# Mixture-of-experts router of a two-layer trunk: logits in four column groups, ranks by five products, gate products moved ahead, loads held back around the row stores and the gathers

## The reference

```python
scores = jax.nn.sigmoid(hf @ w_router)                 # 512 x 16
sel = (scores + router_bias).reshape(t, 4, 4)
group = jnp.argmax(jnp.sum(lax.top_k(sel, 2)[0], axis=-1), axis=-1)
...
_, local = lax.top_k(in_group, TOP_K)                  # two experts of the best group
gate = gate / jnp.sum(gate, axis=-1, keepdims=True)
order = jnp.argsort(flat_e)                            # assignments sorted by expert
...
y = (jax.nn.silu(xblk @ w_gate[e]) * (xblk @ w_up[e])) @ w_down[e]
out = jnp.zeros((t, d)).at[buf_tok].add(yb * buf_w[:, None])
x = x + g_f * out
```

## Time and profile before

| what | us |
|---|---|
| runs | 1720.21, 1727.75, 1726.51 (median 1726.51) |
| the profiled execution, its own time | 1720.86 |
| its span, first to last instruction | 1719.1 |
| PE busy in it | 1476.2 (86%) |
| DVE busy | 667.3 (39%) |
| ACT busy | 306.1 (18%) |
| mean granted clock of TensorE | 0.919 of full |

### The profile page before, as it was taken

How to read it: one execution, slowest core, us unless ns; L and a number is a source line. 1 busy time by engine, 2 the same in 40 slices (tenths; PEclk the granted TensorE clock), 3 DMA queues, 4 the chain that set the end, 5 groups by cost and what they waited for, 6 DMA issues and landing times.

```text
span 1719.1 us, 22464 instructions
## 1 busy us (share of the span) xinstructions
PE 1476.2 (86%) x9809; PEld 767.3 (45%) x9809; DVE 667.3 (39%) x1030; ACT 306.1 (18%) x498; POOL 73.2 (4%) x201
## 2 busy tenths in 40 slices
PE   5999999958887976999999599989559869999992
PEld 2445555437666434333333445655343343333331
DVE  1114433246774234332233235554572352233334
ACT  2121221133331030000000221211220300000002
POOL 7000000000000000000000100000000000000001
PEclk9999999969998996999999799989679878999997
DMA  9686662030001057898988610111000578989984
GB/s 334 201 290 228 213 201 93 1 147 3 3 3 51 0 234 289 345 413 318 428 332 330 246 60 26 49 49 50 0 1 0 211 299 336 418 331 406 370 322 167
DMA packets 91502, 335.21 MB, mean 195 GB/s; under 512 B 6552, under 2 KB 37516, under 8 KB 75020
## 3 DMA queue, kind: packets, MB, share of 16 engines
q1 hardware_dynamic: 76880, 287.94, 43.8%
q10 hardware_dynamic: 8476, 23.82, 3.5%
q0 software_dynamic: 6048, 22.02, 3.4%
HBM read 310.70 MB, written 23.07 MB: 194 GB/s over the span
## 4 chain that ended last, share of the span: by engine, by line
PE 73%; DVE 12%; DMA 8%; ACT 5%; issue 1%; POOL 0%; ACTq 0%; DVEq 0%; SPq 0%; POOLq 0%
PE banks L1629 18%; PE banks L1228 15%; PE banks L1651 10%; PE banks L1558 7%; DVE work L1765 4%; PE banks L1261 3%; PE banks L1217 3%; PE banks L1164 3%; DMA work<-in_w_down_dram 2%; DMA work<-h_rows,idx_tok 2%; DMA h_rows<-y_features 2%; PE banks L1612 2%; DVE work L1771 2%; DVE ring L1765 1%; DMA ring<-in_w_ada_dram 1%
## 5 line engine op out<-in xcount | busy, mean ns | idle before, releaser
L1228 PE MATMUL banks<-h_features,ring 128*128 128x512 f32 (+1 forms) x656 | 290.7, 598 | 4.0 <-ACT h_features L865 4.0
L1629 PE MATMUL banks<-ring,work 128*64 128x512 f32 x672 | 236.1, 613 | 2.3 <-issue 2.3
L1629 PE MATMUL banks<-work 128*64 128x512 f32 x512 | 212.3, 595 | 0.0
L1228 PEld LDWEIGHTS banks<-h_features,ring 128*128 128x128 f32 (+1 forms) x656 | 121.4, 189 | 156.1 <-issue 152.7
L1765 DVE TENSOR_TENSOR work<-work,banks 128x256 f32<-128x256 f32 (+2 forms) x90 | 48.5, 561 | 199.3 <-PE banks L1629 145.5
L1558 PE MATMUL banks<-y_features,ring 128*128 128x512 f32 x256 | 115.2, 613 | 8.6 <-DVE small L2246 8.6
L1651 PE MATMUL banks<-work 128*64 128x512 f32 x320 | 112.7, 593 | 0.0
L1765 DVE TENSOR_TENSOR work<-work 128x512 f32<-128x512 f32 (+10 forms) x205 | 103.3, 504 | 14.4 <-ACT work L1054 3.6
L1629 PEld LDWEIGHTS banks<-ring,work 128*64 128x64 f32 x672 | 71.8, 141 | 72.9 <-issue 69.1
L1651 PE MATMUL banks<-ring,work 128*64 128x512 f32 x256 | 98.4, 592 | 0.0
L1629 PE MATMUL banks<-h_features,work 128*64 128x512 f32 x192 | 91.4, 624 | 2.2 <-ACT work L1087 2.2
(11 more groups left out here) (355 smaller groups left out, 1870.1 us busy)
## 6 DMA issues: line engine op xcount, KB each, us to landing
ring<-in_w_up_dram SPq DMA_DIRECT2D x16, 2048.0 KB, 13.0
y_features<-in_w_ada_dram SPq DMA_DIRECT2D x28, 1024.0 KB, 5.6
work<-in_w_down_dram SPq DMA_DIRECT2D x14, 2048.0 KB, 15.8
ring<-in_w_gate_dram SPq DMA_DIRECT2D x12, 2048.0 KB, 11.0
work<-in_w_up_dram SPq DMA_DIRECT2D x10, 2048.0 KB, 13.2
work<-in_w_gate_dram SPq DMA_DIRECT2D x10, 2048.0 KB, 13.1
ring<-in_w_ada_dram SPq DMA_DIRECT2D x8, 2048.0 KB, 11.8
h_features<-in_w_gate_dram SPq DMA_DIRECT2D x8, 2048.0 KB, 9.1
```

Of the source, the lines that this page charges most:

```text
L1228: ins = mm(PS[0:w, b, :], lhsT=W[:, k, c0:c0 + w], rhs=h[:, k, :], start=(k == 0), stop=(k == KD - 1))
L1629: ins = mm(PS[rows, bank, :], lhsT=xt[:, k, rows], rhs=ws[lane][:, k, :], start=(k == 0), stop=(k == KD - 1))
```

## The change

Seven things are changed; both layers run all but the last, which is made once.

1. The logits go to four column groups of 32 columns: tile k goes to group k mod 4, with a 32-wide stationary operand (the 16 columns of tile k and those of k+1, of which only the first 16 count). ACT copies the full bank, and PE adds the four groups while it turns the tokens, by a product with `quarter_sum` (a 128x16 matrix with four ones in a column). ACT takes the Exp of the 128x64 result, before its four row copies.
2. The ranks are five products over `both` as one 80-column operand, padded with zeros, in place of 14.
3. The gate products stand ahead of the wait for the choices, and go to banks 5 and 6.
4. `tokens_of_blocks` stands inside the first round's gate product, after five of its eight steps, where it stood behind all eight.
5. SP waits for the four row stores ahead of load 4 (down weights of expert 0), where it issued it at once.
6. SP waits for gather 1 ahead of load 6, where it waited for gather 0.
7. Constants for the first point are made once at the start (five DVE instructions).

```diff
@@ SP
                     if place < 2:
+                        if part == 2 and place == 0:
+                            sp.wait_ge(sem(f"l{l}_rows_stored"), 16 * NT)
                         src = ws[part][l, place:place + 1]
...
                                 sp.wait_ge(sem("table_ready"), l + 1)
-                                sp.wait_ge(gathered[l][0], 16)
+                                sp.wait_ge(gathered[l][1], 16)
@@ ACT experts
                 act.wait_ge(sem("logits_ready"), 2 * l + 1)
-                act.activation(sgt[0:E, :], PS[0:E, 4, :], ACT.Exp, scale=-1.0).then_inc(sem("logits_exp"), 1)
+                act.activation(sgt, PS[:, 4, :], ACT.Copy).then_inc(sem("logits_exp"), 1)
+                act.wait_ge(sem("logits_ready"), 2 * l + 2)
+                act.activation(sc, PS[:, 7, 0:NT * E].rearrange("p (a b) -> p a b", b=E), ACT.Exp, scale=-1.0)\
+                   .then_inc(sem("logits_exp"), 1)
...
-                act.activation(gate_row, PS[:, 0:2, :], ACT.Copy).then_inc(sem("scaled"), 1)
+                act.activation(gate_row, PS[:, 5:7, :], ACT.Copy).then_inc(sem("scaled"), 1)
@@ PE experts
-                    ins = mm(PS[0:E, 4, :], lhsT=wr[:, k, :], rhs=h[:, k, :], start=(k == 0), stop=(k == KD - 1))
+                    g = k % 4
+                    ins = mm(PS[32 * g:32 * g + 32, 4, :], lhsT=wr[:, k:k + 2, :].rearrange("p a b -> p (a b)"),
+                             rhs=h[:, k, :], start=(k < 4), stop=(k >= 4))
...
-                            ins = tr(PS[:, 7, s * E:(s + 1) * E], sgt[0:E, s * P:(s + 1) * P], ident[0:E, 0:E])
+                            ins = mm(PS[:, 7, s * E:(s + 1) * E], lhsT=sgt[:, s * P:(s + 1) * P], rhs=quarter_sum,
+                                     start=True, stop=True)
...
-                pe.wait_ge(sem("choices_ready"), 3 * l + 1)
-                for t in range(NT):
-                    for s in range(t + 1):
-                        mm(PS[:, 5, t * E:(t + 1) * E], lhsT=(upper if s == t else ones), rhs=both[:, s, :],
-                           start=(s == 0), stop=(s == t))
-                for s in range(NT):
-                    ins = mm(PS[:, 5, NT * E:(NT + 1) * E], lhsT=ones, rhs=both[:, s, :], start=(s == 0), stop=(s == NT - 1))
-                ins.then_inc(sem("rank_ready"), 1)
-                pe.wait_ge(sem("rows_copied"), NT * l + NT - 1)
                 for k in range(KD):
-                    ins = mm(PS[:, k // 4, (k % 4) * P:(k % 4 + 1) * P],
+                    ins = mm(PS[:, 5 + k // 4, (k % 4) * P:(k % 4 + 1) * P],
                              lhsT=mod[:, l, 40 + k:41 + k].to_broadcast([P, P]), rhs=ident, start=True, stop=True)
                 ins.then_inc(sem("comb_turned"), 1)
+                pe.wait_ge(sem("choices_ready"), 3 * l + 1)
+                every = both_padded.rearrange("p a b -> p (a b)")
+                mm(PS[:, 4, 0:(NT + 1) * E], lhsT=upper, rhs=every, start=True, stop=False)
+                for later in range(1, NT + 1):
+                    ins = mm(PS[:, 4, later * E:(NT + 1) * E], lhsT=ones, rhs=every[:, 0:(NT + 1 - later) * E],
+                             start=False, stop=(later == NT))
+                ins.then_inc(sem("rank_ready"), 1)
...
                     lanes_up(0, ws, xTb[r % 2], range(5))
                     if r:
                         turn_act(r - 1)
+                    else:
+                        tokens_of_blocks()
                     lanes_up(0, ws, xTb[r % 2], range(5, KD)).then_inc(sem(f"l{l}_gate_done"), 1)
                     if r:
...
-                    else:
-                        tokens_of_blocks()
@@ DVE choose
-                dve.wait_ge(sem("logits_ready"), 2 * l + 2)
-                link(tsc(sc, PS[:, 7, 0:NT * E].rearrange("p (a b) -> p a b", b=E), 1.0, ALU.add))
-                link(dve.reciprocal(sc, sc))
+                link(dve.memset(both_padded[:, NT, :], 0.0))
+                dve.wait_ge(sem("logits_exp"), 2 * l + 2)
+                sigmoid_tail(sc)
```

More of the change, by code:

```diff
@@ L192, in trunk @@
         alup = small(256)
-        wr = small(8, E)
+        wr = small(9, E)
+        quarter_sum = small(E)
         rs = work[:, 20480:20992]
@@ L305, in trunk @@
         oh = ro(2, NT * E)
-        both = ro(NT, E)
+        both_padded = ro(NT + 1, E)
+        both = both_padded[:, 0:NT, :]
         gk = ro(2, NT)
@@ L2310, in choose @@
                 dve.wait_ge(sem("rank_ready"), 3 * l + 1)
-                link(tt(rank, PS[:, 5, 0:NT * E].rearrange("p (a b) -> p a b", b=E), both, ALU.subtract))
+                link(tt(rank, PS[:, 4, 0:NT * E].rearrange("p (a b) -> p a b", b=E), both, ALU.subtract))
                 link(stt(rank_first, both[:, :, 0:2], -1024.0, rank[:, :, 0:2], ALU.mult, ALU.add))
```

15 lines of the change are left out of this document (11 added, 4 removed).

## The result

The changed kernel takes **1709.2 us** (median of 8 runs, 1703.8 to 1713.2), the kernel before took 1726.1 beside it (8 runs, 1715.0 to 1728.4). The ratio is 0.991, with a 95% interval of 0.9885 to 0.9936: 11 to 20 us faster. The forecast was 1704, the range 1692 to 1716.

A forecast was written before the change was run, and what follows sets the result against it. Bound: each layer's router waits between the last normalised tile and round 1. Gains of 8.8 + 1.0 = 9.8 us a layer, 19.6 in both, took 1720.86 to 1701.3, placed at 1704 towards the run median; range 1692 to 1716.

The forecast's parts named there:

- Logits: Router logits in four column groups: only the last tile's product remains behind ACT's last tile, ending 3.0 us earlier.
- Ranks and gate products: Router: ten rank instructions take 2.0 us, not 5.7; moving the gate products saves 2.3; first rows known 8.0 earlier.
- Row stores: Before gather 0: without loads 4 and 5 in the way, the last store lands 10.9 us earlier, at 646.0.
- Gather 0: Ahead of round 0: released by the first rows at 646.9, takes 9.7 us beside loads, lands 5.0 earlier.
- Gather 1 and load 6: Ahead of round 1: gather takes 4.4 us, not 11.25; PE waits 2.1 for load 6; round 1 starts 8.8 earlier.
- Clock: Round 1's start: of 2.6 us lost to the low clock, 1.0 a layer is won back.
- thin cover: Loads in later rounds: the tightest one's slack shrinks from 8.4 to 3.6 us, still enough that PE does not wait.
- little contention: Rival: gather 0 needs only 4.4 us and the clock stays up; about 1690 us; chance 0.12.
- the column groups in line: Rival: the logits' column groups do not run beside each other, losing 3.0 us a layer; 1710 us; chance 0.04.
- Full contention: Rival: gather 0 takes 11.3 us and the clock falls as before; about 1709 us; chance 0.16.
- The stream of loads: Rival: loads starting 4.7 us later become the bound, so PE gains only 5 a layer; 1714 us; chance 0.08.
- the slow clock in round 0: Rival: PE stays at 1.2 GHz in round 0, 3.9 us slower a layer; 1731 us; chance 0.05.

The follow-up runs named there:

- e7_logits_as_before: Changed kernel with the logits in one column group again and Exp and token turning as before; 1714.0 us in one run.
- e8_ranks_as_before: Changed kernel with the ranks by 28 instructions again and the gate products behind them; 1721.7 us in one run.
- e1_no_store_hold: Changed kernel with loads 4 and 5 issued at once, no longer waiting for the row stores; 1708.0 us in one run.
- e4_hold_for_gather: Changed kernel with loads 4 and 5 waiting for gather 0 to land instead of the row stores; 1702.5 us in one run.
- e2_no_gather_hold: Changed kernel with load 6 waiting for gather 0, as before, instead of gather 1; 1692.3 us in one run.
- e5_fill: Changed kernel with four unread products of 512 columns added on PE in front of round 1; 1708.5 us in one run.
- e9_load6_first_timed: Changed kernel with loads 4 and 5 behind gather 0, load 6 behind the table alone, load 7 onward behind gather 1; 1687.8 us, ratio 0.980 to the kernel before.
- e12_all_but_holds: Changed kernel with both holds undone (loads 4 and 5 at once, load 6 behind gather 0); 1706.4 us in one run.
- e11_holds_alone: Kernel before the change with only the two holds added (row stores before load 4, gather 1 before load 6); 1725.9 us in one run.
- e6_load6_first: Changed kernel, first run with loads 4 and 5 behind gather 0, load 6 behind the table alone, load 7 onward behind gather 1; 1693.5 us.

## Why the prediction was right, and where it was not

The direction was right, the time lies inside the range, and the line of waits came out in the forecast's order, with load 6 at its end. But the sum was too large: the stretches gained 13.8 where it said 19.6, two steps of it failed (the landing of the row stores and the clock), and the hold for gather 1, which the sum counted as a gain, cost 5.1 us in each layer. That 1709.2 still lies within 6 us of 1704 is in part luck, since the medians moved 3.1 us more than the stretches. Step by step, in layer 0 unless two numbers stand:

- **Logits.** Predicted 3.0 earlier, measured 3.48. The groups run beside each other, and ACT's tiles set the pace: the last logits product ends 1.1 behind ACT's last tile. The Trainium skill, page TensorEngine Tiling (Array Packing), section Theoretical Speedup, allows up to four times, which would be some 2.4 (an estimate); this trace has 5.99. But `e7_logits_as_before` shows that 1.2 / 0.6 is all that counts, since the stores have a pace of their own.
- **Ranks and gate products.** The first rows are known 19.6 behind t0, 1.5 earlier than predicted (646.6 - 625.45 = 21.15). Half of that was won before the ranks began (the logits 0.5, adding the groups 0.8 where I charged 1.0), half in them: they take 1.3 and not 2.0, at a clock of 1.00. In layer 1 they take 2.3 at 0.51, and the first rows are known at 21.3. `e8_ranks_as_before` puts the worth of this part at 3.7.
- **Row stores: the step that failed most.** I divided the bytes taken away (4.2 MB) by 384 GB/s and took all 10.9 us off the landing. The bytes were right: from t0 to the landing 12.57 MB moved before (399 GB/s, share 0.96) and 8.41 after. At 399 that is 21.1 us behind t0. It took 22.9, at a mean of 367 GB/s and a share of 0.90: 406 GB/s up to 652, and 25 in the last 2.3 us. Bytes over a bandwidth leave such an end out. It is no accident of this run: in the ten other kernels that hold loads 4 and 5 back the share in the last 2.3 us ahead of the landing in layer 0 is 0.08 to 0.18, while it is 0.45 in the kernel before and 0.64 in `e1_no_store_hold`, where loads 4 and 5 are there to fill it. (I said that storing is not slower than loading, and 383 GB/s from 642 to 652, half of it stores, does not speak against it.) The landing came 2.3 late (2.0 in layer 1). The forecast also had the wrong releaser: gather 0 was to wait for the first rows at 21.15, and it waited for the stores. So it went out 1.7 late, and round 1 began 1.9 late.
- **Gather 0** beside loads 4 and 5: predicted 9.7, measured 9.8 / 8.9. The rows were the better guide. The Trainium skill, page DMA: Bandwidth & Descriptors, section Queues, rings and completion order, says that an engine takes turns between its queues, from which the prediction made an estimate of 7.2; this trace does not agree. What I missed is that this contention is avoidable at no cost (`e4_hold_for_gather`).
- **Round 0.** The token products came 5.82 behind the gate product, predicted 5.8; in layer 1 6.58, at a mean clock of 0.65 there and 0.74 in layer 0. DVE's third signal held nobody.
- **Gather 1 and load 6.** The gather took 4.1 (4.4), load 6 was issued at 49.3 (48.0), and PE waited 3.35 for it, where I had 2.1. The new wait was foreseen. What I did not see is that the old collision was gone without the hold; I counted the 11.25 of before as what the hold removes, and `e2_no_gather_hold` says that it removes 1.0 / 1.8.
- **Clock: the second step that failed.** I took 1.0 as won back between 0 and 2.6, a choice between the two ends with no row behind it. Nothing was: 10.41 / 10.67 from round 1 to the down product, against 10.34 / 10.26 before. My own sign of being wrong, more than six steps at 0.50, came true in layer 1, where seven steps were slow (six in layer 0, and the seventh in part). `e5_fill` turns it round: without the idle time it takes 7.75. The Trainium skill, page TensorE: Matmul & The Clock Gate, section HAM oscillation, warns that a PE that waits for a DMA is throttled again, and this trace agrees.
- **Later loads.** No wait for a load in the rounds from 2 on, as predicted. The thin cover held; it holds in the version of `e9_load6_first_timed` too. What the forecast did not look at is the last pass behind the rounds, where PE waits for a down load, 3.0 us for both layers in the kernel before and 0.9 in the changed one.

The shortfall of 3.0 in the stretch of layer 0 is 1.9 at round 1 (stores 1.7, and the parts of a microsecond behind them) and 1.1 from the clock; in layer 1 it is 2.8, 1.4 and 1.4. The medians moved by 16.9. The shorter wait in the last passes (2.1 in these two profiles) and the scatter ahead of the routers may explain the difference to 13.8, but these runs do not exclude another cause.

The rivals: little contention and the column groups in line are refuted. Full contention named 1709, the number measured, which lies just outside the 1697 to 1708 that the forecast had claimed for itself. Half of its mechanism came true: the clock fell as before, but gather 0 took 9.8 and not 11.3, and the late landing of the stores, which it did not have, made up the rest. The stream of loads and the slow clock in round 0 did not occur.

## What to carry to other kernels

Where a small gather meets large loads, ask who goes out how many microseconds ahead of it, after all parts of the change are in. A hold paid against loads released together with the gather (3.2 / 3.6 in `e4_hold_for_gather`) and only cost against loads issued 10 us ahead (5.1 in `e2_no_gather_hold`). Release a load by the landing of the small transfer, not by the event that starts it, and do not hold back the one load that is wanted next. When a wait of PE is traded for another of 3 us, count the low clock behind it too.

## What the runs showed of the hardware

- The last 0.06 MB of 2.1 MB of stores took 2.3 us, at a DMA share of 0.06, which is one engine's of the sixteen. Why they are behind the rest no run here tells.
- The landing of the last store did not depend on when it was issued, 13.3 or 16.9 behind t0 in layer 0: 22.9 in both.
- A gather takes 4.0 to 4.8 us with no load beside it. Beside loads it depends on how far ahead they were issued: 4.1 with 4.2 MB issued 10.9 and 11.0 us ahead (`e12_all_but_holds`), 5.1 to 6.1 with 4.2 MB issued 8.7 to 10.5 ahead, 6.8 and 7.2 with 7.2 and 7.3 ahead (`e11_holds_alone`), 7.4 to 7.8 beside one load issued 4.6 to 4.9 ahead (with loads 4 and 5 before it), 9.0 and 9.4 with 4.2 MB issued 4.4 and 5.5 ahead (`e8_ranks_as_before`), 8.9 to 9.9 beside 4.2 MB released together with it or up to 1.5 ahead, and 11.3 beside loads issued 6.9, 6.4 and 1.4 ahead.
- Where PE was busy up to an idle time of 1.1 us in front of round 1, it took 7.75 us from there to the down product. In seven kernels PE waited 2.95 to 7.75 us there for load 6, and the same work took 9.3 to 10.7.
- One and the same program (`e6_load6_first`, `e9_load6_first_timed`) ran an untouched part at a mean clock of 0.90 in one execution and of 1.00 in another, and reached its first router 6.7 us later in the first: more than several of the parts tested here are worth.
